# Where and when the first sample's key pages are loaded in a hybrid attention step

## The reference

```python
q, k, v, ga, qi, ki, wi, u, gb = project(x, pos, w_in)          # D = 2048
# A: an indexer scores all causal keys, each query keeps the best 128 (prompt) or 256 (samples)
scores = einsum('bths,bth->bts', relu(einsum('bthd,bsd->bths', qi, ki)), wi) * scale
p = softmax(where(chosen, q @ k_all.T * 128**-0.5, -inf)); a = p @ v_all
# B: trailing means over 2/4/8/16 positions minus the token, then a 256x256 map for each group
pooled = mean_w(u) - u; p = (pooled @ w_pool) * pool_scale
y = LayerNorm(alpha * x + [a * silu(ga) ; p * silu(gb)] @ w_out) * ln_g + ln_b
```

## Time and profile before

| | us |
|---|---|
| median of 3 runs | 1264.05 |
| the profiled execution | 1260.42 |
| its span | 1258.6 |
| TensorE busy in it | 1192.5 |
| VectorE busy | 597.2 |
| ScalarE busy | 358.8 |
| GpSimd busy | 351.0 |
| DMA | 170.42 MB, mean 135 GB/s |

### The profile page before, as it was taken

One profiled execution on the slowest core, in us unless ns is written; L12 is line 12 of the kernel. 1 busy time (PEld: TensorE's weight loads), 2 busy tenths in 40 slices (PEclk: granted clock), 3 DMA queues, 4 the chain that ended last, 5 costly groups with the idle time before them and its releaser, 6 DMA issues.

```text
span 1258.6 us, 26804 instructions
## 1 busy us (share of the span) xinstructions
PE 1192.5 (95%) x10300; PEld 1097.3 (87%) x10300; DVE 597.2 (47%) x1080; ACT 358.8 (29%) x664; POOL 351.0 (28%) x150
## 2 busy tenths in 40 slices
PE   6899999997999999899997899999999999999995
PEld 6777789997998999899995788988888889999992
DVE  3455567895429514761663432532522652222226
ACT  4233234213322222233232323332232342222210
POOL 2322332333333233333420212212221223434320
PEclk9899999998999899999998999999999999999996
DMA  8522242232333233222405866767766757222203
GB/s 245 137 79 79 57 106 64 77 93 60 86 84 82 72 87 108 76 77 77 126 11 190 272 230 242 264 233 257 262 237 219 239 168 260 84 83 83 67 1 142
DMA packets 197970, 170.42 MB, mean 135 GB/s; under 512 B 19890, under 2 KB 178538, under 8 KB 196658
## 3 DMA queue, kind: packets, MB, share of 16 engines
q1 hardware_dynamic: 184458, 160.48, 41.0%
q10 hardware_dynamic: 13424, 8.67, 2.3%
HBM read 159.47 MB, written 9.74 MB: 134 GB/s over the span
## 4 chain that ended last, share of the span: by engine, by line
PE 76%; DVE 15%; issue 5%; DMA 2%; SPq 1%; ACT 1%; DVEq 0%; ACTq 0%
PE acc L1073 55%; PE bank L1336 4%; PE acc L1424 3%; PE bank L1353 2%; PE bank L1130 2%; DVE rot L1609 2%; DVE scoreP L1686 2%; DVE top L1723 1%; PE bank L1258 1%; PE acc L1478 1%; DVE top L1682 1%; DVE scoreS L1726 1%; DVE rot L1607 1%; DVE kT L1610 1%; PE acc L1382 1%
## 5 line engine op out<-in xcount | busy, mean ns | idle before, releaser
L610 POOL TENSOR_TENSOR wL<-rawW,wH 128x1024 fp32r<-128x1024 f32 (+1 forms) x146 | 350.8, 2404 | 859.2 <-ACT wH L632 859.2
L1073 PE MATMUL acc<-actH,wH 128*128 128x272 f32 (+1 forms) x2304 | 494.9, 296 | 1.2 <-DVE actL L1600 1.2
L1073 PE MATMUL acc<-actH,wL 128*128 128x272 f32 (+1 forms) x2304 | 479.1, 290 | 0.0
L1073 PE MATMUL acc<-actL,wH 128*128 128x272 f32 (+1 forms) x2304 | 477.9, 289 | 0.0
L1073 PEld LDWEIGHTS acc<-actH,wH 128*128 128x128 f32 (+1 forms) x2304 | 363.5, 190 | 25.8 <-issue 23.7
L1073 PEld LDWEIGHTS acc<-actL,wH 128*128 128x128 f32 (+1 forms) x2304 | 364.1, 189 | 0.0
L1073 PEld LDWEIGHTS acc<-actH,wL 128*128 128x128 f32 (+1 forms) x2304 | 361.8, 190 | 0.0
L632 ACT ACTIVATE wH<-rawW 128x1024 fp32r<-128x1024 f32 (+1 forms) x146 | 153.6, 1054 | 214.6 <-PE acc L1073 198.2
L1336 PE MATMUL bank<-sq,kPage 128*128 128x128 f32 x512 | 70.9, 283 | 8.7 <-DMA kPage<-in_cache_k 4.7
L1336 PEld LDWEIGHTS bank<-sq,kPage 128*128 128x128 f32 x512 | 57.0, 144 | 21.8 <-issue 10.9
L1638 DVE SCALAR_TENSOR_TENSOR scoreP<-relu,wiN,scoreP 128x256 f32<-128x256 f32 (+2 forms) x54 | 40.7, 792 | 66.1 <-ACT relu L689 66.1
(11 more groups left out here) (203 smaller groups left out, 1015.7 us busy)
## 6 DMA issues: line engine op xcount, KB each, us to landing
rawW<-in_w_in SPq DMA_DIRECT2D x112, 512.0 KB, 3.8
kPage<-in_cache_k SPq DMA_DIRECT2D x64, 512.0 KB, 4.7
vPage<-in_cache_v SPq DMA_DIRECT2D x64, 512.0 KB, 5.0
rawW<-in_w_out SPq DMA_DIRECT2D x32, 512.0 KB, 3.9
y<-in_x_prompt SPq DMA_DIRECT2D x4, 1024.0 KB, 8.6
out_y_prompt<-y SPq DMA_DIRECT2D x8, 512.0 KB, 2.8
xnat<-in_x_prompt SPq DMA_DIRECT2D x2, 1024.0 KB, 7.6
xnat<-in_x_prompt ACTq DMA_DIRECT2D x2, 1024.0 KB, 11.3
```

Of the source, the lines that this page charges most:

```text
L610: pool.tensor_tensor(wL[:, slot, :, 0:width], rawW[:, slot, :, 0:width], wH[:, slot, :, 0:width].bitcast(F32), ALU.subtract).then_inc(stag ...
L1073: last = pe.matmul(acc[t.slot][0:width, e, 0:HT], w[:, u.slot, k, 0:width], a[:, kk, e * HT:(e + 1) * HT], start=(half == 0 and k == 0 and ...
```

## The change

The four pairs of key pages of sample 0 no longer take turns in the two slots of kPage. Pair 0 goes to kPage's second half, pair 3 to its first, pair 1 and the first page of pair 2 to channels 8 to 13 of mixed, which are not written before the pooling results come, and the second page of pair 2 to raw. Each pair has its own semaphore (first_k_in). Pairs 0 to 2 are issued between the weight loads of TILE_C + 28 to 31, with waits on kidx_sent and the bank of Sn (moved forward), on gate_ready at 8 ahead of the page that goes to raw, and on exp_ready at 1 ahead of value page 0, which now comes before the two U tiles. Pair 3 and value pages 1 and 2 come when exp_ready is 32. Behind c_done the order is wtab, mask, unit 4, the first pair of the second sample (behind K3a instead of K11a), value page 3, unit 5, pool loads, the second pair (behind K15a), units 6 and 7.

```diff
+            def first_keys(pair, e):
+                if pair == 1 or (pair, e) == (2, 0):
+                    at = H * T + (2 * (pair - 1) + e) * H * P
+                    return mixed[:].rearrange("p k t -> p (k t)")[:, at:at + H * P]
+                if pair == 2:
+                    return raw[:].rearrange("p a t -> p (a t)")[:, 0:H * P]
+                return kPage[:, 1 - pair // 3, e, :, :].rearrange("p h d -> p (h d)")
...
-            for j, (col, X) in enumerate(order[:4]):
-                load_tile(w_view, col + (6 + X) * P, TILE_C + 28 + j)
-            for j in range(2):
-                load_tile(w_view, U0 + j * P, TILE_B + j)
...
+            def first_key_page(pair, e):
+                load_page(ck, first_keys(pair, e), page_number(ck, 2 * pair + e), first_k_in[pair])
...
-            b = zb("Sn")
-            sp.wait_ge(bank_free[b.slot], b.read)
-            sp.wait_ge(kidx_sent, 32)
-            key_pages(0, 0, None)
+            (col, X), *others = order[:4]
+            load_tile(w_view, col + (6 + X) * P, TILE_C + 28)
+            first_key_page(1, 0)
+            first_key_page(1, 1)
+            for j, (col, X) in enumerate(others):
+                load_tile(w_view, col + (6 + X) * P, TILE_C + 29 + j)
+                if j == 0:
+                    first_key_page(2, 0)
+                    b = zb("Sn")
+                    sp.wait_ge(bank_free[b.slot], b.read)
+                    sp.wait_ge(kidx_sent, 32)
+                    first_key_page(0, 0)
+                if j == 1:
+                    first_key_page(0, 1)
+                    sp.wait_ge(gate_ready, H)
+                    first_key_page(2, 1)
+                if j == 2:
+                    sp.wait_ge(exp_ready, 1)
+                    value_page(0, 0)
+            for j in range(2):
+                load_tile(w_view, U0 + j * P, TILE_B + j)
 
             sp.wait_ge(exp_ready, 32)
-            key_pages(0, 1, None)
+            first_key_page(3, 0)
+            first_key_page(3, 1)
+            value_page(0, 1)
+            value_page(0, 2)
             sp.wait_ge(c_done, 1)
-            key_pages(0, 2, "K3a")
             sp.dma_start(wtab[:], windows).then_inc(wtab_in, 16)
             mask(0, None)
-            key_pages(0, 3, "K7a")
             unit(4)
-            value_page(0, 0)
-            value_page(0, 1)
+            key_pages(1, 0, "K3a")
+            value_page(0, 3)
             unit(5)
-            key_pages(1, 0, "K11a")
-            unit(6)
-            value_page(0, 2)
             pool_loads(0)
             key_pages(1, 1, "K15a")
+            unit(6)
             unit(7)
-            value_page(0, 3)
...
                 if m % 2 == 0:
-                    pe.wait_ge(k_in[k.slot], 32 * k.full)
+                    if X == "a":
+                        pe.wait_ge(first_k_in[m // 2], 32)
+                    else:
+                        pe.wait_ge(k_in[k.slot], 32 * (k.full - 2))
```

More of the change, by code:

```diff
@@ L312, in layer_program @@
         pad_ready = sem("pad_ready")
+        first_k_in = sems("first_k_in", 4)
         k_in = sems("k_in", 2)
@@ L1334, in keys_turned @@
                     for e in range(2):
+                        h = 2 * (n % 4) + e
                         for a in range(2):
-                            last = pe.transpose(dst[:, (2 * e + a) * P:(2 * e + a + 1) * P],
-                                                kPage[:, 1 - k.slot, a, 2 * (n % 4) + e, :], ident)
+                            page = first_keys(m // 2, a) if X == "a" else kPage[:, 1 - k.slot, a, :, :].rearrange("p h d -> p (h d)")
+                            last = pe.transpose(dst[:, (2 * e + a) * P:(2 * e + a + 1) * P], page[:, h * P:(h + 1) * P], ident)
                     full(b, last)
```

## The result

The changed kernel takes 1252.41 us (median of 4 runs, 1251.45 to 1254.32) beside 1264.51 for the kernel before on the same chip: ratio 0.9906, 95% interval 0.9889 to 0.9923, which is 9.7 to 14.0 us less, 11.9 at the ratio itself. The direction was right and the four waits were the right ones and rightly sized; two other terms failed, what the slow clock behind the waits costs and the carrying over of one profile's saving to the medians.

The account below looks back on a forecast made before the run. TensorE, busy 95%, was taken as the bound. Waits of 7.52 us plus 1.19 of clock, less 0.1 and 0.1, gave 8.5 us: 1264.05 to 1255.5 us, with an 8-in-10 range of 1253 to 1259.

Parts of the forecast that it names:

- the four waits: TensorE between 667 and 700 us: key pages 1.30 and 1.89, second sample's page 1.54, history 2.79; all 7.52 us go.
- charge for the copies: VectorE's copies out of the two banks, with the mask operation, may come late in the stage: 0 to 0.2 us, 0.1 taken.
- new wait on gate_ready: On SP's queue in the last pair: delays the last Q tile's load, with 6 us left, so it costs nothing.
- four late pages: Two key and two value pages in flight from about 660 us may delay the dropD store: 0 to about 1 us, 0.1 taken.
- Rival C: Key turning stage and after: the granted clock stays low, up to 13.1 us more, slower at 1268.7 us; chance 0.03.
- factor 0.87: 1.90/1.02 less 1, the low clock's extra on two quarters of a unit, within a 6.1 us cost behind the stage.
- A: Part of the waits returns elsewhere, at the history, dropD store or VectorE; half the 8.5 us stays, 1259.8 us; chance 0.08.
- B: Nothing is won: the page waits are truly for something else, such as masks or VectorE; 1264 us, chance 0.05.
- D: A weight tile comes late behind the gate_ready wait, needing a landing of 15 us instead of 9.1; slower, chance 0.01.
- sign of being wrong: At the first turning of key pages: the forecast is wrong if the turning stage begins later than 667.5 us.
- the clock term: Behind the history wait, 24 matmuls take 4.20 us where the next take 3.01; the 1.19 us come back.
- the anchor: The 8.5 us saving from the profiled 1260.42 us execution should be the same in the median, 1264.05 us.

Follow-up runs that it names:

- the last kernel above: early_copy with the first sample's pool loads moved right behind wtab, ahead of the masks; 1246.07 us, ratio 0.9863 to the kernel before.
- hist_late: Changed kernel with the first sample's pool loads moved behind unit 6, so the history is late again; 1257.68 us, ratio 0.9958 to the kernel before.
- b_again: The kernel before, unchanged, profiled a second time and timed against itself; 1263.84 us, ratio 1.0001.
- b_third: The kernel before, unchanged, profiled a third time; 1263.05 us.
- hist_first: Kernel before with only the first sample's pool loads moved right behind the wait for c_done; 1257.94 us, ratio 0.9961.
- order_only: Kernel before with value pages earlier and pool loads ahead of the second sample's pages, key pages keeping kPage's two slots; 1259.07 us, ratio 0.9961.
- early_copy: Changed kernel with VectorE's first two key copies ahead of its store wait, masked sum behind all copies; 1248.92 us, ratio 0.9895 to the kernel before.

## Why the prediction was right and where it was too small

*Right.* The bound: TensorE, with DMA waits in this one place. The two key page waits (3.19 us) went: from the first turning to the quarter behind the stage's new keys the profiles have 23.1 us before (667.5 to 690.6) and 19.9 after (668.6 to 688.5). The second sample's page and the history followed. The steps from the fourth turning on are 1.56 to 1.59 us apart but for one, 682.64 to 684.37, which takes 1.73. There VectorE's mask operation stands ahead of its copy, as the prediction saw, and this is its charge for the copies (0.1 taken, 0.14 measured): in the last kernel above, where the mask comes behind all copies, the same step takes 1.59. So the copies do keep pace. The new wait on gate_ready held SP for 7.8 us and cost nothing: its page left at 597.73 and the weight unit at 598.21, and from the last make_gate (596.19, have 595.11) to the first turning it is 72.4 us in both kernels. The four late pages did run on until about 670 us (256 GB/s from 666 to 668 us, where the earlier trace rows have 0), and VectorE's wait for the store grew from 1.70 to 1.74 us; 0.1 was allowed.

```profile
672.02 0.94 DVE L1844 MEMSET probS<- 128x1056 f32 x1 [1.74 <-DMA dropD<-scoreS]
...
682.92 0.69 DVE L1867 CUSTOM_DVE_ANT_0 probS<-bank,probS 128x512 f32<-128x512 f32 x1 [0.48 <-PE bank L1381]
...
683.53 0.69 DVE L1856 COPY mixed<-bank 128x512 f32<-128x512 f32 x1
```

(The last two are the mask operation and the copy behind it.)

Rival C, the clock that doesn't rise, is refuted: from 683 to 686 us the changed kernel has 1.00 with TensorE busy in 2.94 of 3.00 us. The sentence of the Trainium skill on transposes (TensorE: Matmul & The Clock Gate, Part 4) is again not borne out for this mix of turnings and products. (That case's factor 0.87 is 0.86 by its own rows, which leaves its 6.1 us as they are.) Nor did A, B or D occur. One sign of being wrong did: the first turning began at 668.59, later than 667.5. But the kernel before itself has 669.8 and 667.8 in its other profiles, so this sign could not tell a cost of the change from chance.

*Too small: the clock term.* This is the step that failed. "4.20 − 3.01 = 1.19 us come back" was one quarter's loss in one execution, and I took it for a constant. The low clock cost 1.34, 2.67 and 3.51 us in three profiles of before, mean 2.5, and all that the stage held over and above the waits 1.73, 3.07 and 3.97, mean 2.9. hist_late shows by itself that a wait of 2.78 us brings 1.68 us more. The first profile's own loss was close to the 1.19 (1.34; its second quarter behind the history was at full speed again), so the fault was less in the reading than in taking one mild execution for all. Another 0.4 us in the steps with waits had no term. The four waits were sized well (7.52 forecast, 7.52, 7.98 and 7.60 measured). With the mean of three the stage's gain is 45.7 − 35.1 = 10.6 us, where 8.5 were forecast (44.4 to 35.9) and 9.25 lie between the first profile of either kernel.

*Too small: the anchor.* "The saving should be the same in it" carried an execution of 1260.42 us over to a median of 1264.05. The 3.6 us between them were a hint that the profiled execution was a mild one, and that part of what it lacked lay behind the very waits to be removed. b_again, at 1264.5, has 1.8 us of its 4.1 more in the stage and 2.3 ahead of it; b_third, at 1263.05, has 2.3 of its 2.6 in the stage. The range went 2.5 us below the forecast, and no case in it had the gain larger; it should have had one.

*Open.* 10.6 us of stage against 11.9 in the ratio of the runs: the difference lies within the interval (from 9.7). What is left may come from the stretch ahead of the first turning, which took 667.5, 669.8 and 667.8 us in the profiles of before and 668.6 and 668.7 in those of after. With so few profiles I can't tell a difference there from chance. What decides how long the clock stays low behind a given wait isn't shown either. In the stages of the profiles above, no wait of TensorE for a load that lasted 2.58 us or less had a loss behind it (2.58 in hist_first, 2.54 in order_only, 2.10 in early_copy). The six longer ones all had one, but its size doesn't follow their length: 2.78 us brought 1.5 more behind it, 2.79 brought 1.3, 2.91 1.15, 3.15 2.4, 3.19 1.5 and 3.43 2.7.

## What to carry to other kernels

Where many loads go out in a fixed order just ahead of their use, a load that is moved out of that stretch also helps those behind it: the key pages' new places alone won most of the gain (10.2 of 11.9 us), the new order alone under half (4.9). Price a wait of TensorE by its length and by what the clock loses behind it, which here was nothing behind the shorter waits and 1.15 to 2.7 us behind each of the longer. Take this from several profiles: the one that was read for the forecast, 3.6 us faster than the median, had the smallest of these losses (1.3 in all, where the others had 2.7 and 3.5). When the front of a stage is made faster, ask at once which load was only just in time before; here it was the history, and one moved line took another 2.3 us out of the stage.

## What the runs showed of the hardware

Profiled executions of the kernel before differ by up to 2.3 us before any of this begins (first turning at 667.5, 669.8 and 667.8 us). Stretches from 20 to 40 us of the first profile of before, of b_again and of the changed kernel, in this order:

```profile
20.00:40.00 20.00, 17.41 (x140) 17.02 (x139) 5.84 (x9) 4.84 (x9) 10.09 (x5) 1.00 0.56 154
```

```profile
20.00:40.00 20.00, 17.06 (x125) 16.43 (x124) 4.29 (x10) 6.12 (x11) 9.45 (x5) 0.89 0.55 152
```

```profile
20.00:40.00 20.00, 17.26 (x117) 16.87 (x118) 3.01 (x9) 5.27 (x10) 8.74 (x5) 0.83 0.56 153
```

TensorE was granted a mean clock of 1.00, 0.89 and 0.83 of full speed there, and the one with 1.00 reached the first turning first of the three (667.5, 669.8 and 668.6). The order of the other two, and b_third with 0.83 and 667.8, show that this stretch doesn't settle it; what the start-up costs stays open. A DMA issue on SP takes about 0.4 us as a rule (0.36 for the second of the two history loads in order_only). The first of them took 3.05 us, behind five transfers of 512 KB issued in four us, so even a load of 60 KB issued there delays what is issued behind it.
